# One 512-column product for a block's high part in the down projections

## What is computed

```
def _swiglu(h, wg, wu, wd):
    return (jax.nn.silu(h @ wg) * (h @ wu)) @ wd
...
x = x + swiglu(...)          # first block, layers 0 and 1
...
x = x + g2 * _swiglu(h, ffn_gate[l], ffn_up[l], ffn_down[l])   # second block, layers 0 and 1
```

## Time and profile before

| | |
|---|---|
| three executions | 1255.08, 1255.6, 1257.1 us, median 1255.6 |
| span of the profiled execution | 1254.2 us |
| PE busy | 1194.7 us, 95% |
| VectorE busy | 927.1 us, 74% |
| ScalarE busy | 657.7 us, 52% |
| mean granted TensorE clock | 0.990 of 2.4 GHz |
| moved from and to HBM | 258.10 MB, mean 206 GB/s |

### The profile page before, as it was taken

How to read it: one execution, slowest core, us unless ns; L and a number is a source line. 1 busy time by engine, 2 the same in 40 slices (tenths; PEclk the granted TensorE clock), 3 DMA queues, 4 the chain that set the end, 5 groups by cost and what they waited for, 6 DMA issues and landing times.

```text
span 1254.2 us, 24815 instructions
## 1 busy us (share of the span) xinstructions
PE 1194.7 (95%) x9914; PEld 1138.3 (91%) x9914; DVE 927.1 (74%) x1761; ACT 657.7 (52%) x1143; POOL 80.8 (6%) x91
## 2 busy tenths in 40 slices
PE   7898999999999999999997889999999889999999
PEld 7778999999987999999987779999998778999999
DVE  6547798878777888788788758888885566766652
ACT  6336654445446644445555766444444776545431
POOL 2021000001000100002100011000000222000000
PEclk9999999999999999999999989999999999999999
DMA  8862688878753587788643436877776433655552
GB/s 287 237 169 85 235 303 261 255 256 282 260 190 122 193 271 253 239 262 270 236 138 123 123 101 202 270 255 254 254 280 205 139 110 92 214 185 183 185 185 68
DMA packets 81414, 258.10 MB, mean 206 GB/s; under 512 B 9032, under 2 KB 22164, under 8 KB 81300
## 3 DMA queue, kind: packets, MB, share of 16 engines
q1 hardware_dynamic: 75540, 250.69, 60.6%
q10 hardware_dynamic: 5760, 5.83, 1.8%
HBM read 253.82 MB, written 2.67 MB: 205 GB/s over the span
## 4 chain that ended last, share of the span: by engine, by line
PE 79%; DVE 9%; ACT 4%; issue 3%; DMA 1%; POOL 1%; ACTq 0%; DVEq 0%; POOLq 0%
PE ps L527 72%; DVE wlo L1273 2%; PE ps L578 1%; PE ps L641 1%; PE ps L645 1%; PE ps L636 1%; DVE X L1279 1%; PE ps L637 1%; DMA uscr<-U 1%; DVE aacc L1279 1%; DMA UR<-uscr 1%; ACT whi L864 1%; ACT HH L864 1%; DVE HL L1279 1%; ACT oS L864 1%
## 5 line engine op out<-in xcount | busy, mean ns | idle before, releaser
L527 PE MATMUL ps<-HH,whi 128*128 128x256 f32 (+1 forms) x2152 | 620.7, 288 | 16.9 <-DVE wlo L1273 7.6
L527 PE MATMUL ps<-HH,wlo 128*128 128x256 f32 (+1 forms) x2152 | 611.4, 284 | 0.0
L527 PE MATMUL ps<-HL,whi 128*128 128x256 f32 (+1 forms) x2152 | 610.8, 284 | 0.0
L864 ACT ACTIVATE whi<-raw 128x1024 fp32r<-128x1024 f32 (+1 forms) x364 | 382.6, 1055 | 347.1 <-PE ps L527 331.7
L1273 DVE TENSOR_TENSOR wlo<-raw,whi 128x1024 fp32r<-128x1024 f32 (+1 forms) x364 | 442.0, 1221 | 46.5 <-ACT whi L864 46.0
L527 PEld LDWEIGHTS ps<-HH,whi 128*128 128x128 f32 x2152 | 411.1, 191 | 34.0 <-issue 23.9
L527 PEld LDWEIGHTS ps<-HL,whi 128*128 128x128 f32 x2152 | 411.2, 191 | 0.4
L527 PEld LDWEIGHTS ps<-HH,wlo 128*128 128x128 f32 x2152 | 410.9, 191 | 0.0
L527 PE MATMUL ps<-GH,whi 128*128 128x256 f32 x704 | 197.9, 281 | 0.6 <-DVE bcol L1498 0.5
L527 PE MATMUL ps<-GL,whi 128*128 128x256 f32 x704 | 197.3, 280 | 0.0
L527 PE MATMUL ps<-GH,wlo 128*128 128x256 f32 x704 | 197.3, 280 | 0.0
(11 more groups left out here) (220 smaller groups left out, 933.0 us busy)
## 6 DMA issues: line engine op xcount, KB each, us to landing
raw<-wall SPq DMA_DIRECT2D x363, 512.0 KB, 4.3
araw<-ada SPq DMA_DIRECT2D x96, 512.0 KB, 4.7
UR<-uscr ACTq DMA_DIRECT2D x32, 142.0 KB, 3.7
oBB<-kbias SPq DMA_DIRECT2D x16, 192.0 KB, 2.5
aTB<-scratch SPq DMA_DIRECT2D x12, 128.0 KB
uscr<-U ACTq DMA_DIRECT2D x8, 143.5 KB, 4.6
out<-X SPq DMA_DIRECT2D x8, 128.0 KB, 2.8
aTB<-scratch SPq DMA_DIRECT2D x12, 64.0 KB
```

The costliest lines, as they stand in the source:

```text
L527: ins = pe.e.matmul(o, l, r, start=(kt == p.order[0] and i == 0), stop=(kt == p.order[-1] and i == 2))
L864: ac.then_inc(ac.e.activation(o, i, func, **kw), sem)
```

## The change

For the first seven of the eight tiles of each down projection, `GH` and `GL` become halves of one tile `GB[P, 22, 2, T]`. The matmul of high weights takes both halves of a block row as one operand of 512 columns and writes all 512 columns of the bank: the first 256 collect the products with the high activations, the other 256 those with the low ones. The matmul of the low weights with the high activations follows, into the first 256 columns. At the end of such a tile VectorE adds columns 256 to 511 to `X`, waits for itself, and then adds columns 0 to 255 as before. The eighth tile is computed as before.

```
-            GH, GL = sb("GH", [P, KF, T], F32R, st), sb("GL", [P, KF, T], F32R, st)
+            GB = sb("GB", [P, KF, 2, T], F32R, st)
+            GH, GL = GB[:, :, 0, :], GB[:, :, 1, :]
...
+        def halves(name, nt):
+
+            return PROD[name].kts == KF and nt < PROD[name].tiles - 1
...
+                        elif halves(name, nt):
+
+                            pe.e.matmul(ps[:, :].rearrange("p (a t) -> p a t", a=2), wh, GB[:, kt, :, :],
+                                        start=(kt == p.order[0]), stop=False)
+                            ins = pe.e.matmul(ps[:, 0:T], wl, hh[:, kt, :], start=False, stop=(kt == p.order[-1]))
+                            mm = []
...
                         dv.wait_ge(S.hl, 8 * j + nt + 1)
+                    if halves(name, nt):
+
+                        stt(X[:, nt, :], ps[:, T:2 * T], scale(nt), X[:, nt, :], op, ALU.add, S.xlow)
+                        dv.settle()
                     stt(X[:, nt, :], ps[:, 0:T], scale(nt), X[:, nt, :], op, ALU.add, S.ev)
```

More of the change, by code:

```diff
@@ L345, in __init__ @@
         self.hi0, self.lo0 = new("hi0"), new("lo0")
-        self.hh, self.hl = new("hh"), new("hl")
+        self.hh, self.hl, self.xlow = new("hh"), new("hl"), new("xlow")
         self.sq, self.sqa, self.tot = new("sq"), new("sqa"), new("tot")
```

## The result

Median of twenty runs of each: 1257.21 us before, 1252.09 us after. The ratio is 0.996 with a 95% interval of 0.9946 to 0.9974, so the change makes the kernel 5.1 us faster, between 3.3 and 6.8. I had forecast 13.5 and a range of 1239 to 1249.5: right sign, less than half the size.

The account below looks back on a forecast made before the run. TensorE's matmul stream was taken to bound the down projections; savings of 3.4 + 3.2 + 3.7 + 3.2 = 13.5 us, all else at nothing, gave 1242.1 us. Its own range was 1240 to 1244, with other cases 1239 to 1249.5.

Parts of the forecast that it names:

- What bounds the kernel: Down projections: only TensorE's matmul stream sets the time; what it gains the stage gains, as long as suppliers keep up.
- The row used: fp32 matmuls of line 584, 128x128 weights, 256 columns: 215 ns each, 213.3 of it streaming, taken as the long matmul's price.
- The pace before: Matmul to matmul in the down projections before the change: 118.7, 117.9, 119.4 and 117.9 ns in dn0 to dn3.
- The pair of rows that spoke against it: Two other stages: 118.1 ns with 256 columns, 120.0 with 258; if only the load counted, nothing would change.
- Rival 1: Down projections: each matmul costs its columns plus a fixed 11 ns; saving 7.3 us, 1248.3 us, chance 0.20.
- No gain in the stream: Down projections: cost goes with columns, so one 512-column matmul takes as long as two of 256; 1255.6 us, chance 0.09.
- the unhidden load: Down projections: the low weights' load waits for the long matmul's end; 52 us slower, 1307 us, chance 0.06.
- Rival 2: Down projections: cost proportional to columns, saving 0, 1255.6 us; by the isolated-gap formula 1254.1; chance 0.09.
- VectorE's addition at nothing: End of seven tiles per down projection: 28 extra additions, 12.6 us of engine time, all hidden; 12.6 to 15.4 us if not.
- The suppliers: VectorE, ScalarE and DMA feeding the down projections 5% faster, costed at nothing; rival loses 6.9 us, 1249.0 us, chance 0.07.
- the eighth tile: Last tile of each down projection: left as it is, its addition being on the path to next stage and output.
- the stages behind: Stages after the down projections: move as a whole, no longer than before; last matmul to kernel end unchanged at 2.8 us.

Follow-up runs that it names:

- the streams: Kernels of matmuls alone, one form at a time with a fresh load each, varying width, type and operand place: fp32r 113.4 to 121.5 ns at 256 columns.
- the two strip kernels: 160 unused bytes per partition allocated ahead of the operands, in the kernel before (0.9976, 1255.59 us) and in the changed kernel (0.9964, 1253.65 us).
- two experiments: Changed kernel with TensorE's part undone, additions kept: 0.9992, 1256.4 us; changed kernel with VectorE's second addition left out: 0.9963, 1253.38 us.
- the first stream kernel: Standalone fp32r matmuls, 48 per width from 64 to 512 columns, then fp32 and others' traffic: 120.1 ns at 256 columns, 227.7 at 512.

## Why the prediction was wrong, point by point

- **What bounds the kernel**: right. The projections are one unbroken stream of matmuls before and after, and the gain is what the stream gained.
- **The step that failed** is "I take it that a 128-column load with its exchange is what lasts 118 ns, and that a matmul whose columns last longer than that costs its columns and some 2 ns ... its price is 215 ns." A load's pace is 108 ns, and the long matmul costs 228.6 to 230.0. In the sum that turned 20.7 to 23.9 ns a block into 5.2 to 9.3, 13.5 us into 4.5; the long matmul, some 14 ns under its cost, makes 8.8 of the missing 9 us. The row used was read rightly, and its streams were repeated with the same 215.8 ns; but fp32 takes two cycles for a column and fp32r one, and the 11 ns I wanted to explain exist only in the second. I had called the cycles the same and treated the type as no difference.
- **The pace before** was read a little high in three of the four: the length of a chain piece runs to the end of its last matmul, and dn2 has three pieces. From start to start dn1 and dn3 have 117.3 ns, not 117.9, and dn2 118.7, not 119.4. That made the forecast saving too large by some 0.6 us.
- **The pair of rows that spoke against it** deserved its weight, since a pace that changes with two more columns can't be a load's pace. But it was weak evidence: the streams show that places alone move the pace by more than its 1.9 ns.
- **Rival 1** had the right kind, a cost that belongs to each fp32r matmul. Its size, 7.3 us, supposed that the cost stays at 11 ns for 512 columns; in the kernel it is 15 to 17. With that the saving is 2 x 117.3 - 230.0 = 4.6 ns a block in dn3, and 0.7 more because the short matmul behind the long one takes 116.6; in dn0 it is 2 x 118.7 - 228.6 = 8.8, and 0.6 more.
- **No gain in the stream, the unhidden load**: out. The load of the low weights hides, as the 229 ns of the long matmul and the falling PEld share show. Rival 2's size, no saving at all, is what the two strip kernels show in three projections.
- **VectorE's addition at nothing**: right for one (two experiments), and the reserve behind it measured: two more per tile cost 15.8 us. The forecast of 90% of VectorE's time in dn1 was 53.0/61.8 = 86%, but the second half stands at 94%.
- **The suppliers, the eighth tile, the stages behind**: as forecast. ScalarE still waited for TensorE in dn1, and from the last matmul to the end nothing changed.

**Open** is what in the reading of a 4-byte operand costs 7 to 15 ns at 256 columns and 13 to 25 at 512. Shown: it is not other engines' or DMA's traffic, nor the bank, nor the shape of the operand, nor the number of rows; shorter loads relieve 256 columns and not 512; the places of operand and weights move it by up to 8 ns, and not the same way twice. So the size of the gain belongs to this placement and is no property of the long matmul. The ends of matmuls are modelled in the trace; all this rests on starts.

## What to carry to other kernels

Before pricing a matmul by another row of the trace, match the element type and the cycles per column as well as the widths and loads; if no such row exists, keep both prices in the range at their full weight. Joining two matmuls on the same weights into one saves at most the cost that each has beside its columns, here 5 to 9 ns of a block's 352 to 356 and with 160 bytes ahead of the operands mostly nothing: the load was already hidden. Divide starts by starts: the length of a chain piece holds the tail of its last matmul. When an engine that is 85% busy gets more work, look at its fullest stretch and at the wait behind the stage, not at its mean and not inside the stage: the debt shows up where the next stage starts.

## What the runs showed of the hardware that I had not expected

- bf16 and fp32 matmuls back to back cost 2.4 to 2.5 ns beside their columns, fp32r matmuls 7 to 21 ns, with every other engine of the core silent, and up to 25 in the kernel.
- Matmuls of 64, 96 and 128 columns run at the same 108 ns, the pace of a 128-column load.
- The pace of a 256-column fp32r stream lies anywhere from 113.4 to 121.5 ns with the places of its operands; 160 unused bytes ahead of the operands moved the long matmul of the kernel from 229 or 230 ns to between 232 and 238.
- Streams of 64 to 192 columns ran at 147 to 214 ns in the first stream kernel, where the granted clock had sunk to 0.50, the level of 1.2 GHz, during the 64-column stream; in the second, between wide ones, the same streams ran at 108 to 111 ns with the clock at 1.00.
